# The first unit pair of a two-layer transformer kernel, fed from a transposed copy of x

## The chip, the core and the metric

One core of a Trainium2 chip. The metric is the device time of one execution in microseconds (us), median of several runs. The engines are TensorE (PE, with its weight loads PEld), VectorE (DVE), ScalarE (ACT), GpSimd (POOL) and SyncE (SP), which only issues DMAs here; ScalarE issues DMAs too.

## The reference, cut to what matters

The program is two layers of feed-forward, retention and gated delta rule, cross attention and feed-forward, then a third block, for 256 tokens of width 1024 in float32. What the change touches is the very first sublayer:

```
y = x * rsqrt(mean(x * x, axis=-1) + 1e-6)
u = y * norm_pre[0, 0]
h = (silu(u @ w_gate) * (u @ w_up)) @ w_down      # ffn1, 1024 -> 2816 -> 1024
```

The root belongs to a token (a row of x), the norm's weight ("gain" below) to a column. So u @ w is the token's root times ((x * gain) @ w).

## The kernel before, in words

All weights come as 297 units of 128 x 2048 floats (1 MB). SP loads them in order into a ring of 5 landing buffers (`raw`). Every product is made of three: each operand is split into a high part (`whi`, `uT[0]`, rounded to fp32r) and a low part (the remainder), and high x high, high x low and low x high are added up in PSUM. ScalarE makes a unit's high part (128x2048 copy), POOL its low part in place of the landed unit (four instructions of 128x512, line 391), TensorE multiplies and counts the unit as done, which frees its buffer for SP's next load.

The first feed-forward is worked in chunks of 256 hidden columns. Chunk 0 is one "pair" of units, 0 and 1: the top and bottom 512 rows of 512 columns, 256 of the gate and 256 of the up projection, multiplied by token (TensorE's stationary operand is a block of u, `first_pair`). Bank 0 holds tokens 0 to 127, bank 1 the rest. ScalarE takes Silu of the gate half and VectorE multiplies it with the up half, once per bank (`chunk_by_token`). Chunk 1 follows by rows: `rows_unit` for unit 2 (gate), then `h_transposes` of chunk 0's two products on TensorE, then `rows_unit` for unit 3 (up), then unit 4 (down projection).

Every engine has its instructions in one fixed, hand-written order; semaphores hold them. At the start of the kernel before:

- SP issues x's first token half, the identity, units 0 and 1 in halves with x's second half between them, unit 2, the tables (constants, positions, masks), and units 3 on.
- ScalarE issues the norm's weight as one row, then squares x's first half with a sum per token (`first_root`), takes the root, splits half of unit 0, copies the transposed u (`u_hi`), and so on with the second half; then it splits units 2 and 3, issues five DMAs (three rows, the memory, the small constants), and does chunk 0's Silus with unit 4's split between them.
- VectorE takes the reciprocal, scales x into u (`first_scale`; the norm's row comes spread over 128 partitions from a TensorE product with a row of ones), makes unit 0's low part (`first_lo`, line 1173) and u's low parts (`u_lo`, line 1181).
- POOL skips unit 0 and starts with unit 1.
- TensorE does 9 idle products (line 2247, of zeros, into a bank that is not yet used), the row products (2253), transposes of u (2040), and the pair in parts as the data come (2081, 2098, 2074, 2076, 2088), with 6 idle products between them.

Of the kernel before, what the change touches and what calls it, by code (L numbers as in the profile page):

```python
# [23 lines left out]
P = 128  # L24
# [88 lines left out]

class Prog:
# [19 lines left out]
def build(nc, a, out):  # L134
    ctx = ExitStack()
    with ctx:
# [57 lines left out]
        one_row = arena[0:1, 0:P]  # L194
# [23 lines left out]
        tmpn = view(8240, NT, D)  # L218
# [118 lines left out]
        def _(sp):  # L337
            p = Prog(sp)
            sp.dma_start(x[:, 0, :], a["x"][:, 0, :]).then_inc(sems["x_in0"], 16)
            sp.dma_start(cst[:, 0:P], a["cst"][:, 0:P]).then_inc(sems["ident_in"], 16)  # L340
            for n in range(2):
                for half in range(2):
                    k = slice(half * UNIT // 2, (half + 1) * UNIT // 2)
                    sp.dma_start(raw[n][:, k], a["w"][n][:, k]).then_inc(sems[f"raw_{('first', 'landed')[half]}{n}"], 16)
                if n == 0:
                    sp.dma_start(x[:, 1, :], a["x"][:, 1, :]).then_inc(sems["x_in1"], 16)
            sp.dma_start(raw[2][:], a["w"][2]).then_inc(sems["raw_landed2"], 16)
            sp.dma_start(cst[:, P:], a["cst"][:, P:]).then_inc(sems["tables_in"], 16)
# [3 lines left out]
            for n in range(3, N_UNITS):  # L352
# [11 lines left out]
        def _(pool):  # L364
# [20 lines left out]
            for n in range(N_UNITS):  # L385
                pool.wait_ge(sems["w_hi"], p.count("w_hi"))
                if n == 0:
                    continue
                for c in range(0, UNIT, UNIT // 4):
# [4 lines left out]
                if n == 8:  # L394
                    pool.wait_ge(sems["tables_in"], 48)
                    for i, m in enumerate((UI, UI, LI, LI)):
                        pool.tensor_copy(msk4[:, i, :], m)
                    pool.wait_ge(sems["tables_in"], 48)
# [18 lines left out]
        def _(act):  # L417
# [23 lines left out]
            def row():  # L441

                r = state["row"]
                if r < N_ROWS:
                    if r == 0:
                        act.dma_start(rows[0:1, 0, :], a["rows"][0:1, :]).then_inc(sems["row_landed0"], 16)
                    else:
# [50 lines left out]
            def first_root(t):  # L498

                act.wait_ge(sems[f"x_in{t}"], 16)  # L500
                fn(junk, x[:, t, :], AF.Square, accum_out=st[:, 48 + t:49 + t])
                root(st[:, 54 + t:55 + t], st[:, 48 + t:49 + t], D).then_inc(sems["rms_pre"], 1)
# [55 lines left out]
            def chunk_by_token(u0, c):  # L558
# [5 lines left out]
                for t in range(NT):  # L564
# [4 lines left out]
                    fn(sg[q][:, t * 256:(t + 1) * 256], bank[b[t]][:, 0:256], AF.Silu).then_inc(sems["silu_gate"], 1)  # L569
# [66 lines left out]
            for L in range(DEPTH):  # L636
                base = L * LAYER_UNITS
                if L == 0:
                    first_root(0)
                    first_split(0, (0,))  # L640
                    u_hi(0)
                    first_split(0, (1,))
                    first_root(1)
                    first_split(1)
                    state["split"] = 2
                    u_hi(1)
                    split(2)
# [35 lines left out]
                if L == 0:  # L683
                    act.wait_ge(sems["tables_in"], 48)
# [443 lines left out]
        def _(dve):  # L1128
# [27 lines left out]
            def first_scale(t):  # L1156

                r = st[:, 54 + t:55 + t]
                dve.wait_ge(sems["rms_pre"], p.count("rms_pre"))
                dve.reciprocal(r, r)  # L1160
                dve.drain()
                for h in range(2):
                    c = slice(h * 512, (h + 1) * 512)
                    if t == 0:
                        dve.wait_ge(sems["first_row"], h + 1)
                    stt(ub[:, t, c], bank[2 + h][:, :], r, x[:, t, c], ALU.mult, ALU.mult).then_inc(sems["u_ready"], 1)

            def first_lo(half):

                dve.wait_ge(sems[("w_hi_half", "w_hi")[half]], 1)  # L1170
                for c in range(half * UNIT // 2, (half + 1) * UNIT // 2, UNIT // 4):
                    k = slice(c, c + UNIT // 4)
                    r = tt(wlo[0][:, k], raw[0][:, k], whi[0][:, k].bitcast(F32), ALU.subtract)
                r.then_inc(sems["first_lo"], 1)
# [66 lines left out]
            def ffn(memory=False, tables=None):  # L1241
                for c in range(CH):
                    if c in (0, CH - 1):
                        chunk_by_token(c)
# [5 lines left out]
            def chunk_by_token(c):  # L1250
# [3 lines left out]
                for t in range(NT):  # L1254
                    dve.wait_ge(sems["silu_gate"], p.count("silu_gate"))
                    k = slice(t * 256, (t + 1) * 256)
                    tt(h_tok[q][:, k], sg[q][:, k], bank[b[t]][:, 256:512], ALU.mult).then_inc(sems["ff_product"], 1)
# [26 lines left out]
            dve.memset(one_row, 1.0)  # L1284
            dve.memset(st[:, 0:60], 0.0).then_inc(sems["eps_set"], 1)

            def rotary_angles():

                dve.wait_ge(sems["tables_in"], 48)
                dve.wait_ge(sems["tables_in"], 48)  # L1290
# [44 lines left out]
            for L in range(DEPTH):  # L1335
                base = L * LAYER_UNITS
                if L == 0:
                    state["row"] += 1
                    p.skip("row_landed0", 16)
                    first_scale(0)  # L1340
                    first_lo(0)
                    u_lo(0, 0)
                    u_lo(0, 1)
                    first_lo(1)
                    first_scale(1)
                    u_lo(1, 0)
                    u_lo(1, 1)
                else:
                    boundary()
                ffn(True, None if L else rotary_angles)  # L1350
                if L == 0:
                    dve.wait_ge(sems["trig"], p.count("trig"))
                    ts(sinT[:, :], sinT[:, :], cst[:, C_INV + 1:C_INV + 2], None, ALU.mult)
                boundary()
# [565 lines left out]
        def _(pe):  # L1920
# [40 lines left out]
            def by_rows(b, w, j, parts, start=True, stop=True, low_waited=True):  # L1961
# [3 lines left out]
                for k, c in enumerate(tiles):  # L1965
                    pe.matmul(both, w[0][:, c], parts[:, :, k, :], start=start and k == 0, stop=False)  # L1966
# [6 lines left out]
            def rows_unit(b0):  # L1973
# [956 lines left out]
```

## Time and profile before

| what | us |
|---|---|
| median of 3 runs (lowest, highest) | 1928.16 (1926.05, 1928.46) |
| span of the profiled execution | 1926.1 |
| TensorE busy | 1912.5 (99%) |
| POOL busy | 1545.7 (80%) |
| ScalarE busy | 1081.6 (56%) |
| VectorE busy | 710.4 (37%) |

For the profiled execution the page gives its span and no other time; the three runs stand beside it for comparison. Times inside the trace count from the start of the span. "Chain" is the chain of work that ended last, followed back from the end: each piece is what held up the next. In a timeline, consecutive instructions of one kind are merged; the second figure is from the first one's start to the last one's end.

### The profile page before, as it was taken

How to read it: one execution, taken by the hardware profiler on the slowest of the kernel's cores; microseconds unless marked ns; L12 is line 12 of the kernel's file. 1: busy time of each engine (PE TensorE's matmuls, PEld its weight loads, DVE VectorE, ACT ScalarE, POOL GpSimd, SP SyncE). 2: the span in 40 equal slices, each digit the busy share in tenths (PEclk: the TensorE clock that was granted, in tenths of full speed). 3: DMA queues.
4: the chain of work that ended last, by engine and by line, in shares of the span. 5: the costliest groups of instructions: out<-in, count | busy, mean ns of one | idle time of the engine just before them, and what ended most of it. 6: DMA issues, size and time to landing. Idle time of an engine off the chain costs nothing.

```text
span 1926.1 us, 28361 instructions
## 1 busy us (share of the span) xinstructions
PE 1912.5 (99%) x11293; PEld 1685.0 (87%) x11293; DVE 710.4 (37%) x1428; ACT 1081.6 (56%) x1439; POOL 1545.7 (80%) x1228
## 2 busy tenths in 40 slices
PE   9999999999999999999999999999999999999998
PEld 7888899988888888889999888888999998888887
DVE  2221767521311232128574231113577632122112
ACT  6645684456644575456735565446666667445443
POOL 6998786666899799979776759997767787888995
PEclk9999999999999999999999999999999999999999
DMA  8554543143555565555322535555443444445552
GB/s 321 179 204 175 197 154 132 45 177 130 219 197 183 187 227 205 179 193 186 143 88 105 187 125 207 188 196 202 152 160 145 148 160 153 175 177 206 196 182 103
DMA packets 48661, 331.50 MB, mean 172 GB/s; under 512 B 5393, under 2 KB 6289, under 8 KB 10514
## 3 DMA queue, kind: packets, MB, share of 16 engines
q1 hardware_dynamic: 44208, 314.61, 44.3%
q10 hardware_dynamic: 4322, 15.09, 2.3%
q8 instruction: 89, 1.46, 0.3%
q14 instruction: 42, 0.34, 0.1%
HBM read 328.63 MB, written 1.05 MB: 171 GB/s over the span
## 4 chain that ended last, share of the span: by engine, by line
PE 97%; ACT 1%; DVE 1%; issue 0%; ACTq 0%; DVEq 0%
PE bank L1966 20%; PE bank L1935 16%; PE bank L1936 16%; PE bank L1937 16%; PE bank L1970 10%; PE bank L2074 2%; PE bank L2098 2%; PE bank L2076 1%; PE bank L2412 1%; PE bank L2428 1%; PE bank L2040 1%; PE bank L2534 1%; PE bank L2513 1%; PE bank L2674 1%; PE bank L2088 0%; ACT arena L422 0%
## 5 line engine op out<-in xcount | busy, mean ns | idle before, releaser
L391 POOL TENSOR_TENSOR wlo<-raw,whi 128x512 fp32r<-128x512 f32 x1184 | 1501.0, 1305 | 332.5 <-ACT whi L422 331.9
L422 ACT ACTIVATE whi<-raw 128x2048 fp32r<-128x2048 f32 (+1 forms) x299 | 567.5, 1901 | 188.8 <-PE bank L1937 168.8
L422 ACT ACTIVATE arena<-bank 128x512 f32<-128x512 f32 (+4 forms) x389 | 210.3, 551 | 445.2 <-PE bank L1970 268.4
L1966 PE MATMUL bank<-uT,whi 128*128 128x512 f32 x1632 | 408.2, 392 | 0.0
L1966 PEld LDWEIGHTS bank<-uT,whi 128*128 128x128 f32 x1632 | 296.3, 189 | 55.0
L1970 PEld LDWEIGHTS bank<-uT,wlo 128*128 128x128 f32 x1632 | 222.6, 190 | 15.9
L1970 PE MATMUL bank<-uT,wlo 128*128 128x256 f32 x1632 | 227.6, 282 | 0.0
L1935 PE MATMUL bank<-uT,whi 128*128 128x256 f32 x768 | 222.5, 290 | 0.0
L1936 PE MATMUL bank<-uT,whi 128*128 128x256 f32 x768 | 217.1, 283 | 0.0
L1937 PE MATMUL bank<-uT,wlo 128*128 128x256 f32 x768 | 217.1, 283 | 0.0
L1935 PE MATMUL bank<-whi,uT 128*128 128x512 f32 (+1 forms) x416 | 160.8, 387 | 0.0
L1936 PE MATMUL bank<-wlo,uT 128*128 128x512 f32 (+1 forms) x416 | 158.6, 381 | 0.0
L1937 PE MATMUL bank<-whi,uT 128*128 128x512 f32 (+1 forms) x416 | 158.6, 381 | 0.0
L1935 PE MATMUL bank<-whi,hT_hi 128*128 128x512 f32 x400 | 157.0, 392 | 0.0
L1936 PE MATMUL bank<-wlo,hT_hi 128*128 128x512 f32 x400 | 156.1, 390 | 0.0
L1937 PE MATMUL bank<-whi,hT_lo 128*128 128x512 f32 x400 | 155.8, 389 | 0.0
L1935 PEld LDWEIGHTS bank<-uT,whi 128*128 128x128 f32 x768 | 147.1, 191 | 2.5 <-issue 2.1
L1936 PEld LDWEIGHTS bank<-uT,whi 128*128 128x128 f32 x768 | 147.2, 192 | 1.7 <-issue 1.4
L1937 PEld LDWEIGHTS bank<-uT,wlo 128*128 128x128 f32 x768 | 147.1, 192 | 0.0
L1266 DVE TENSOR_TENSOR bank<-bank,arena 128x512 f32<-128x512 f32 x45 | 31.5, 700 | 312.7 <-ACT arena L422 312.7
L1273 DVE TENSOR_TENSOR bank<-bank,arena 128x512 f32<-128x512 f32 x45 | 31.5, 699 | 190.2 <-ACT arena L422 190.2
L1937 PEld LDWEIGHTS bank<-whi,uT 128*128 128x128 f32 x416 | 78.2, 188 | 15.2
(321 smaller groups left out, 2702.0 us busy)
## 6 DMA issues: line engine op xcount, KB each, us to landing
raw<-in_w SPq DMA_DIRECT2D x295, 1024.0 KB, 4.8
rows<-in_rows ACTq DMA_DIRECT2D x22, 512.0 KB, 4.7
raw<-in_w SPq DMA_DIRECT2D x4, 512.0 KB, 6.7
arena<-in_mem ACTq DMA_DIRECT2D x2, 1024.0 KB, 7.8
x<-in_x SPq DMA_DIRECT2D x2, 512.0 KB, 5.2
arena<-in_amask ACTq DMA_DIRECT2D x1, 576.0 KB, 6.4
out<-x SPq DMA_DIRECT2D x1, 512.0 KB, 2.7
out<-arena SPq DMA_DIRECT2D x1, 512.0 KB, 2.7
```

What stands on the lines that cost most here:

```text
L391: r = pool.tensor_tensor(wlo[n % LAND][:, k], raw[n % LAND][:, k], whi[n % RING][:, k].bitcast(F32), ALU.subtract)
L422: return act.activation(o, i, f, **k)
L1266: tt(gate, gate, gate_low, ALU.add).then_inc(sems["gate_sum"], 1)
L1273: tt(up, up, up_low, ALU.add)
L1935: pe.matmul(o, l[0], r[0], start=start, stop=False)
L1936: pe.matmul(o, l[0], r[1], start=False, stop=False)
L1937: return pe.matmul(o, l[1], r[0], start=False, stop=stop)
L1966: pe.matmul(both, w[0][:, c], parts[:, :, k, :], start=start and k == 0, stop=False)
L1970: r = pe.matmul(both[:, 0], w[1][:, c], parts[:, 0, k, :], start=False, stop=stop and k == KT - 1)
L2040: r = pe.transpose(bank[b][:, k * P:(k + 1) * P], ub[:, t, f:f + P], ident)
L2074: pe.matmul(bank[b][:, :], u, w[0][:, c], start=half == 0 and k == 0, stop=False)
L2098: r = pe.matmul(bank[b][:, :], uT[1][:, 4 * half + k, t * P:(t + 1) * P], w[0][:, k * 512:(k + 1) * 512], start=False, stop=half == 1 and ...
```

## The change: what it does

A second copy of x, transposed (columns on partitions) with the norm's gain in 8 columns ahead of it, is laid out by the host as an input `xT`. The pair of units 0 and 1 is multiplied with x times gain, split into high and low parts in the buffer of the memory's transposes (`mT`), for both token banks at once. The token's root is applied to the pair's results: as the scale of Silu and as a factor of the product with the up half. The sum of squares is formed from the squares of xT: added up over the 8 column blocks on VectorE, then over partitions by TensorE products with ones, once per token down the partitions and once as a row spread over all of them (`row_root`). With that row VectorE forms u (transposed, in place), ScalarE copies its high part and VectorE subtracts for its low part, in four steps (`first_u`, `first_u_hi`); unit 2's first pass waits for each step. POOL now makes the low part of the second halves of units 0 and 1, VectorE that of the first halves. x itself is loaded after the tables. The 16 transposes of u, the row products and the 6 idle products between are gone; 13 idle products stand at the start in place of 9.

```diff
 # SP
+            sp.dma_start(x_turned[:, 0:cut], a["xT"][:, 0:cut]).then_inc(sems["turned_in0"], 16)
+            first_weights(0)
+            sp.dma_start(x_turned[:, cut:], a["xT"][:, cut:]).then_inc(sems["turned_in1"], 16)
+            first_weights(1)
+            sp.dma_start(cst[:, 0:2 * P], a["cst"][:, 0:2 * P]).then_inc(sems["ident_in"], 16)
+            for n in range(2, 4):
+                sp.dma_start(raw[n][:], a["w"][n]).then_inc(sems[f"raw_landed{n}"], 16)
...
+            for t in range(NT):
+                sp.dma_start(x[:, t, :], a["x"][:, t, :]).then_inc(sems["tables_in"], 16)
 # POOL
-                if n == 0:
-                    continue
-                for c in range(0, UNIT, UNIT // 4):
+                for c in range(UNIT // 2 if n < 2 else 0, UNIT, UNIT // 4):
 # ScalarE
+            def first_values(half):
+                act.wait_ge(sems[f"turned_in{half}"], 16)
+                for k in range(4 * half, 4 * half + 4):
+                    fn(mT[0][:, k, :], xs[:, k, :], AF.Identity, scale=x_gain[:, k:k + 1]).then_inc(sems["start_act"], 1)
...
+            def first_roots():
+                act.wait_ge(sems["act_bank2"], p.count("act_bank2"))
+                eps = st[:, 60:61]
+                fn(st[:, 54:56], bank[3][:, 0:4:2], AF.Sqrt, scale=1.0 / D, bias=eps).then_inc(sems["start_act"], 1)
+                fn(row_root, bank[2][:, 0:SEQ], AF.Sqrt, scale=1.0 / D, bias=eps).then_inc(sems["start_act"], 1)
+            def first_u_hi():
+                for j in range(4):
+                    act.wait_ge(sems["start_dve"], START_DVE[f"x_scaled{j}"])
+                    fn(uT[0][:, 2 * j:2 * j + 2, :], xs[:, 2 * j:2 * j + 2, :], AF.Copy).then_inc(sems["start_act"], 1)
...
-                    first_root(0)
+                    first_values(0)
                     first_split(0, (0,))
-                    u_hi(0)
+                    first_squares(0)
                     first_split(0, (1,))
-                    first_root(1)
+                    first_values(1)
+                    first_squares(1)
                     first_split(1)
                     state["split"] = 2
-                    u_hi(1)
-                    split(2)
+                    first_roots()
+                    split()
+                    first_u_hi()
+                    split()
 # VectorE
+            def squares_added():
+                s = x_squares
+                dve.wait_ge(sems["start_act"], START_ACT["squares1"])
+                tt(s[:, 4:6], s[:, 4:6], s[:, 6:8], ALU.add)
+                dve.drain()
+                tt(s[:, 0:2], s[:, 0:2], s[:, 4:6], ALU.add)
+                dve.drain()
+                tt(s[:, 0], s[:, 0], s[:, 1], ALU.add).then_inc(sems["start_dve"], 1)
+            def first_u():
+                def scaled(j):
+                    for k in (2 * j, 2 * j + 1):
+                        r = stt(xs[:, k, :], xs[:, k, :], x_gain[:, k:k + 1], row_root, ALU.mult, ALU.mult)
+                    r.then_inc(sems["start_dve"], 1)
+                def lo(j):
+                    k = slice(2 * j, 2 * j + 2)
+                    dve.wait_ge(sems["start_act"], START_ACT[f"u_hi{j}"])
+                    tt(uT[1][:, k, :], xs[:, k, :], uT[0][:, k, :].bitcast(F32), ALU.subtract).then_inc(sems["start_dve"], 1)
+                dve.wait_ge(sems["start_act"], START_ACT["roots"])
+                dve.reciprocal(row_root, row_root)
+                dve.reciprocal(st[:, 54:56], st[:, 54:56]).then_inc(sems["start_dve"], 1)
+                dve.drain()
+                scaled(0)
+                for j in range(1, 4):
+                    scaled(j)
+                    lo(j - 1)
+                lo(3)
...
+                    first_values_lo(0)
                     first_lo(0)
+                    dve.wait_ge(sems["start_act"], START_ACT["squares0"])
+                    tt(x_squares[:, 0:2], x_squares[:, 0:2], x_squares[:, 2:4], ALU.add)
+                    first_values_lo(1)
+                    squares_added()
                     first_lo(1)
+                    first_u()
 # TensorE
+            def first_unit_pair(banks):
+                def product(n, w, values, ks, tiles=(0, 1), stop=False):
+                    for t in tiles:
+                        for k in ks:
+                            r = pe.matmul(bank[banks[t]][:, :], values[:, 4 * n + k, t * P:(t + 1) * P], w[:, k * 512:(k + 1) * 512],
+                                          start=w is whi[0] and values is mT[0] and k == 0, stop=stop and k == ks[-1])
+                    return r
+                pe.wait_ge(sems["start_act"], START_ACT["value3"])
+                pe.wait_ge(sems["w_hi_half"], 1)
+                product(0, whi[0], mT[0], (0, 1))
...
+                product(1, whi[1], mT[0], (0, 1))
+                pe.wait_ge(sems["ident_in"], 16)
+                pe.wait_ge(sems["start_dve"], START_DVE["squares_added"])
+                for t in range(NT):
+                    pe.matmul(bank[3][:, 2 * t:2 * t + 2], x_squares[:, 0, t * P:(t + 1) * P], ones[:, 0:2], start=True, stop=True)
+                pe.matmul(bank[2][:, 0:SEQ], ones, x_squares[:, 0, :], start=True, stop=True).then_inc(sems["act_bank2"], 1)
+                pe.wait_ge(sems["start_dve"], START_DVE["values_lo1"])
+                product(1, whi[1], mT[1], (0, 1))
...
                 for k, c in enumerate(tiles):
+                    if first and k % 2 == 0:
+                        pe.wait_ge(sems["start_dve"], START_DVE[f"u_lo{k // 2}"])
                     pe.matmul(both, w[0][:, c], parts[:, :, k, :], start=start and k == 0, stop=False)
...
-            idle_products(9)
-            pe.wait_ge(sems["row_landed0"], 16)
+            idle_products(13)
```

`first_values_lo(half)` is four VectorE instructions of 128x256, (x * gain) - high part, each waiting for its value. `START_ACT` and `START_DVE` are tables of counts of the two start semaphores.

## Rows read from the trace of the kernel before

**Rows 1.** The page: busy shares, TensorE's granted clock, the chain by engine.
```profile
PE 1912.5 (99%) x11293; PEld 1685.0 (87%) x11293; DVE 710.4 (37%) x1428; ACT 1081.6 (56%) x1439; POOL 1545.7 (80%) x1228
...
PEclk9999999999999999999999999999999999999999
...
PE 97%; ACT 1%; DVE 1%; issue 0%; ACTq 0%; DVEq 0%
```
**Rows 2.** The chain of waits, first 45 us: start, us, what.
```profile
1.71 4.21 PE bank L2247 x9
...
26.47 1.81 PE bank L1966 x8
28.29 0.95 PE bank L1970 x8
...
32.03 0.44 PE bank L2192 x4
32.47 1.85 PE bank L1966 x8
```
**Rows 3.** ScalarE's timeline to 34 us: start, us, engine, line, operation, out<-in, count.
```profile
4.86 1.06 ACT L422 ACTIVATE arena<-x 128x1024 f32<-128x1024 f32 x1 [2.06 <-DMA x<-in_x]
...
20.13 1.92 ACT L422 ACTIVATE whi<-raw 128x2048 fp32r<-128x2048 f32 x1
20.63 0.36 ACTq L448 DMA_DIRECT2D rows<-in_rows  x1
21.03 0.93 ACTq L651 DMA_DIRECT2D arena<-in_mem  x1
...
21.99 1.50 ACTq L448 DMA_DIRECT2D rows<-in_rows  x2
23.52 1.23 ACTq L655 DMA_DIRECT2D small<-in_small  x1
24.78 1.28 ACT L422 ACT_TABLE_LOAD   x1 [0.93 <-issue]
26.08 0.39 ACT L422 ACTIVATE arena<-bank 128x256 f32<-128x256 f32 x1
26.36 1.91 ACT L422 ACTIVATE whi<-raw 128x2048 fp32r<-128x2048 f32 x1
28.16 0.37 ACT L422 ACTIVATE arena<-bank 128x256 f32<-128x256 f32 x1
```
**Rows 4.** Line 344's two loads of unit 1's halves, issued at 3.05 and 3.55.
```profile
L344 SPq DMA_DIRECT2D raw<-in_w x2: 452/487/522, 3.1 to 3.6; - x2
...
DMA to landing us min/median/max: 7.9/8.3/8.6
```
**Rows 5.** VectorE's groups by line and form, whole span: count | busy us, mean ns.
```profile
L1266 DVE TENSOR_TENSOR bank<-bank,arena 128x512 f32<-128x512 f32 x45 | 31.5, 700 | 312.7 <-ACT arena L422 312.7
...
L1173 DVE TENSOR_TENSOR wlo<-raw,whi 128x512 fp32r<-128x512 f32 x4 | 2.6, 686 | 0.3 <-ACT whi L422 0.3
...
L1627 DVE RECIPROCAL st<-st 128x2 f32<-128x2 f32 x8 | 1.3, 166 | 13.5 <-ACT arena L422 13.5
...
L1305 DVE SCALAR_TENSOR_TENSOR bank<-arena,bank 128x256 f32<-128x256 f32 x3 | 1.3, 429 | 0.2
...
L1464 DVE RECIPROCAL gat<-gat 128x16 f32<-128x16 f32 x2 | 0.5, 246 | 0.0
```
**Rows 6.** ScalarE's groups by line and form, whole span: copies with a column scale.
```profile
L422 ACT ACTIVATE arena<-arena,st 128x256 f32<-128x256 f32 x16 | 7.3, 503 | 0.9 <-DVE st L1627 0.9
```
**Rows 7.** POOL's line 391 to 22 us: ns min/median/max, first and last start.
```profile
L391 POOL TENSOR_TENSOR wlo<-raw,whi x4: 1282/1290/1305, 16.6 to 20.3; 128x512 fp32r<-128x512 f32 x4
```
**Rows 8.** VectorE's line 1774 and POOL's line 391 from 1506 us on, as rows 7.
```profile
L1774 DVE TENSOR_TENSOR arena<-arena x2: 693/1241/1789, 1506.2 to 1506.8; 128x512 f32<-128x512 f32 x2
...
L391 POOL TENSOR_TENSOR wlo<-raw,whi x4: 1610/1738/1760, 1506.5 to 1511.4; 128x512 fp32r<-128x512 f32 x4
```
**Rows 9.** Line 448, the rows' DMA issues, whole span: as rows 7.
```profile
L448 ACTq DMA_DIRECT2D rows<-in_rows x22: 334/352/845, 20.6 to 1741.9; - x22
```

More of the change, by code:

```diff
@@ L111, in rope_tables @@
     return np.concatenate([np.concatenate([cos, cos]), np.concatenate([-sin, sin])], axis=1).astype(np.float32)
+START_ACT = {f"value{k}": k + 1 + k // 4 for k in range(KT)}
+START_ACT.update(squares0=5, squares1=10, roots=12, u_hi0=13, u_hi1=14, u_hi2=15, u_hi3=16)
+START_DVE = {"values_lo0": 1, "weights_lo0": 2, "values_lo1": 3, "squares_added": 4, "weights_lo1": 5, "recip": 6}
+START_DVE.update(x_scaled0=7, x_scaled1=8, u_lo0=9, x_scaled2=10, u_lo1=11, x_scaled3=12, u_lo2=13, u_lo3=14)
 class Prog:
@@ L568, in chunk_by_token @@
                         act.wait_ge(sems["unit_done"], u0 + (1, 29)[c // (CH - 1)] + 1)
-                    fn(sg[q][:, t * 256:(t + 1) * 256], bank[b[t]][:, 0:256], AF.Silu).then_inc(sems["silu_gate"], 1)
+                    first = u0 == 0 and c == 0
+                    if first and t == 0:
+                        act.wait_ge(sems["start_dve"], START_DVE["recip"])
+                    fn(sg[q][:, t * 256:(t + 1) * 256], bank[b[t]][:, 0:256], AF.Silu,
+                       scale=st[:, 54 + t:55 + t] if first else 1.0).then_inc(sems["silu_gate"], 1)
                     if c == 0 and t == 0:
@@ L1168, in first_lo, with first_values_lo @@
[L1168 to L1174, printed above, removed]
+            def first_values_lo(half):
+                for k in range(4 * half, 4 * half + 4):
+                    dve.wait_ge(sems["start_act"], START_ACT[f"value{k}"])
+                    r = stt(mT[1][:, k, :], xs[:, k, :], x_gain[:, k:k + 1], mT[0][:, k, :].bitcast(F32), ALU.mult, ALU.subtract)
+                r.then_inc(sems["start_dve"], 1)
@@ L1239, in lo_parts, with ffn @@
                        ALU.subtract).then_inc(sems[f"dve_read{b}"], 1)
-            def ffn(memory=False, tables=None):
+            def ffn(memory=False, tables=None, first=False):
                 for c in range(CH):
                     if c in (0, CH - 1):
-                        chunk_by_token(c)
+                        chunk_by_token(c, first and c == 0)
                     else:
@@ L1959, in proj_T, with by_rows @@
                 r.then_inc(sems["unit_done"], 1)
-            def by_rows(b, w, j, parts, start=True, stop=True, low_waited=True):
+            def by_rows(b, w, j, parts, start=True, stop=True, low_waited=True, first=False):
                 both = bank[b].rearrange("p (a b) -> p a b", a=2)
@@ L2126, in first_pair @@
[L2126 to L2147 removed]
+                    first_unit_pair(banks)
@@ new lines, in first_pair @@
+                    return
+                wa = unit()
+                acquire(a, readers[0])
+                hi_phase(wa, a, 0, 0)
+                lo_phase(wa, a, 0, 0)
+                m = state["unit"]
+                state["unit"] += 1
+                wb = whi[m % RING], wlo[m % LAND]
+                pe.wait_ge(sems["w_hi"], m + 1)
+                hi_phase(wb, a, 0, 1, True)
+                weights_lo_phase(wb, a, 0, 1, False)
+                lo_phase(wb, a, 0, 1).then_inc(sems["tok_half"], 1)
@@ L2249, in _ @@
             pe.wait_ge(sems["eps_set"], 1)
-            idle_products(9)
-            pe.wait_ge(sems["row_landed0"], 16)
-            for h in range(2):
-                pe.matmul(bank[2 + h][:, :], one_row, rows[0:1, 0, h * 512:(h + 1) * 512], start=True, stop=True)\
-                    .then_inc(sems["first_row"], 1)
+            idle_products(13)
             for L in range(DEPTH):
@@ L2870, in pack @@
     assert n == N_UNITS
+    turned = f["x"][0].T.reshape(KT, P, SEQ).transpose(1, 0, 2).reshape(P, KT * SEQ)
+    gain = f["norm_pre"][0, 0].reshape(KT, P).T
     tiled = lambda m: np.ascontiguousarray(m.reshape(NT, P, D).transpose(1, 0, 2))
     arrays = {
-        "w": w, "small": small, "rows": np.stack(rows), "x": tiled(f["x"][0]), "mem": tiled(f["mem"][0]),
+        "w": w, "small": small, "rows": np.stack(rows), "x": tiled(f["x"][0]), "xT": np.concatenate([gain, turned], axis=1), "mem": tiled(f["mem"][0]),
         "pos": np.ascontiguousarray(f["positions"][0:1]), "cst": shape_constants(), "lvl": level_masks(),
```

152 lines of the change are left out of this document (60 added, 92 removed).

## Prediction

> **What bounds the kernel now.** I read the page's busy shares and chain first, then the chain of waits over the first 45 us, then ScalarE's timeline there. TensorE is busy 99% of the span and holds 97% of the chain [rows 1]. So whatever ends TensorE's first stretch earlier or later moves the end by as much, as long as no later wait swallows it; the question is only at which time TensorE begins steady work. The chain says when: the first unit pair ends and unit 2 begins at 26.47; unit 2 takes 5.56 (two passes of 1.81 and 0.95) and ends at 32.03; four transposes of chunk 0's product take 0.44; unit 3 begins at 32.47 [rows 2]. In all of it TensorE waits for almost nothing, because it was given the pair, the transposes of u and idle products in turn. I use 32.47, the start of unit 3, as the mark: behind it TensorE runs without waiting, so the shift of that start is the shift of the end.
>
> The second thing to see is ScalarE. It splits units 2 and 3, then its queue issues five DMAs (20.63 to 24.75), then it loads the Silu table (24.78, 1.28) and only then reads the pair's first result at 26.08; the split of unit 4 comes between the two Silus, so the second starts at 28.16 [rows 3]. TensorE asks for that second product at 32.03, so this string has 3.5 us of cover now. The change takes the cover and the start of the string in different directions.
>
> **The change part by part.** *Arrivals.* x's first half was read at 4.86 [rows 3]; xT's first half stands in its place with 8 columns more, so 4.9. The last half of raw 1 was issued at 3.55 and landed 8.6 later, at 12.2 [rows 4]; the bytes ahead of it stay the same but for the identity (64 KB later), so it stays at 12.2. Units 2 and 3 come ahead of the tables on SP's queue now and x itself behind them; unit 4 stands behind some 1 MB more than before, but ScalarE asks for it only at 34.0 below, and x and the tables are first read after several units more. Unit 5's load waits for unit 0's end, which comes earlier (13.6).
>
> *ScalarE, first part.* Four scaled copies of 128x256 (a lone one is 0.50 [rows 6]; in a row I take 0.42, the second starting before the first's end is recorded): 4.95 to 6.6. Then half-split, squares, half-split at 1.0 each (1.06 recorded [rows 3]) to 9.6; four copies more to 11.3; squares to 12.3; the halves of unit 1 to 13.3 and 14.3.
>
> *POOL* now also splits half of units 0 and 1: two instructions of 1.29 [rows 7] from 9.75, two from 14.4. Before, it did nothing until 16.6, and VectorE did its low half at 0.69 apiece undisturbed [rows 5, 7].
>
> *VectorE against POOL.* The new VectorE work has both operands in SBUF. What that costs beside POOL [rows 8]: of two equal additions the first took 0.69, the second 1.79, while POOL's four weight instructions of 1.29 took 1.61 to 1.76. The two take turns, one instruction each: a VectorE instruction waits for the running POOL one (1.25), and POOL for it (0.3 to 0.5). One whose operand is in PSUM kept 0.70 over 45 cases with POOL busy [rows 5]. The Trainium skill ("SBUF — State Buffer", Who interferes with whom) has it as an exclusive lock on a shared port, which the instruction that starts first keeps to its end. Read that way alone, a VectorE string without gaps would keep POOL out and pay nothing in the u stage below, and the sum would be an estimated +0.4; the turn-taking [rows 8] says otherwise, and I follow the rows.
>
> *Sum of squares.* The low parts of values 4 to 7 alternate with POOL's two and end at 13.6. The three additions (0.6, 0.6, 0.35 and drains) would end at 14.1; POOL's unit-1 instructions fall among them, and with two turns the last ends at 16.4. The products with ones (two of 2 columns and one of 256, full f32) I put at 1.1 with start and tail, two ScalarE roots 0.6: 18.3. *Unit 2's split* is queued behind the roots on ScalarE, so the added wait for the sums holds it and, behind it, POOL's unit 2: 1.9 [rows 3], 20.2.
>
> *Reciprocal of 256 elements:* no row. From 2 to 16 elements it grows from 0.166 to 0.246, 5.7 ns an element [rows 5], so 1.6; the lower bound is an ordinary 128x256 instruction, 0.43 [rows 5], the upper some 2.1. I take 1.5: 20.2 with the small one 20.4. It hardly counts, for POOL starts unit 2 at 20.3 in either case.
>
> *The u stage.* Eight scalings (0.35) and four subtractions (0.6) are 5.2 alone. POOL's four instructions of unit 2 stand between the first: four turns of 1.25 + 0.25 bring the second scaled pair to 26.4; free of POOL, the rest gives u_lo0 27.0, x_scaled3 29.0, u_lo3 30.4.
>
> *TensorE.* Thirteen idle products at 0.468 (4.21 for nine [rows 2]), fewer if the clock rises among them: about 7.5. Groups of four at 0.91 follow the data: unit 0 done 13.6, the sums 17.6, the pair 22.1, which is 4.3 earlier than 26.47. Unit 2's first pass then waits for u_lo0 to u_lo3, 27.1 to 31.0, and 0.95 + 1.84 + 0.95 bring its end to 34.7 (32.03 before).
>
> *The string behind it.* The sequencer can't issue its DMAs until x_scaled3 lets the last u_hi go: 29.1. Their price: 4.12 in this trace [rows 3]; 1.9 if each takes what later ones take (a rows issue: 0.352 median [rows 9], 0.46 for mem). The rows issues were slow only behind a loaded start, and at 29 us units 4 and 5 are in; I take rows at 0.35 and keep the first-time 0.93 and 1.23: 3.2, to 32.3. Table 1.28, Silu 0.39: 34.0; unit 4's split to 35.9; Silu 36.2; product and transposes, 0.9: unit 3 at about 36.9, against 32.47: **+4.4** (at 1.9, unit 2's own end and Silu give +3.4; at 4.1, +5.3). The skill ("ScalarE: Activation LUTs", What ACT_TABLE_LOAD costs) adds a drain of about 1.38 us to each load, which would make it an estimated +5.8; by the trace [rows 3] Silu starts 0.02 after the load's end, and I add none.
>
> *Behind the mark* POOL is next: it splits unit 4 until 41.9, TensorE asks at 42.5; unit 5 and on are needed later still. Nothing given back, nothing more lost. The second silu's scale and the two-operand product cost as before; leaving out 16 transposes, the row product and the broadcast saves TensorE time that it then spends waiting. POOL's tables wait at unit 8 is long past.
>
> **Forecast:** 4.4 us later. The profiled span is 1926.1 [rows 1], 2.1 under the median of the runs, inside their spread of 2.4; on the median, 1928.2 + 4.4 = **1932.6**.
>
> **Rivals.** (1) *The turns don't bite*: POOL and VectorE mostly miss each other. Then the sums are ready at 15.6, x_scaled3 at 22.1, unit 2 ends at 27.9, the DMAs at 25.4, the second Silu at 29.5, unit 3 at 29.9: -2.6 (-1.6 to -3.5 by the price of the issues), 1925.6: not slower. For it: a turn lost or won moves a whole instruction. Against: POOL has work at exactly those times. It decides at u_lo0: the change breaks even where that comes at 22.6, 4.4 before my 27.0. (2) *The head's whole gain comes through*: the pair ends at 20.1, unit 2 follows without stall and the Silus are in time: -6.4, 1921.8. For it: the pair's work itself shrinks so far. Against: the DMAs and the table stand ahead of the Silu at any time after the last u_hi. (3) *TensorE's clock*: the nine idle products of 0.468 us ran at the 1.2 GHz level and unit 2's at 0.226 at the 2.4 GHz level [rows 2], though the page's granted clock reads full throughout [rows 1], so its row doesn't show the start. TensorE now idles from 22.1 to 27.1; should the clock fall back there, unit 2 costs up to 4 more, of which 2.3 is hidden behind the Silu string: +6 to +8, 1935. (The skill, "TensorE: Matmul & The Clock Gate", Part 1, says that an idle stretch returns the clock to half; no row here shows one.)
>
> **How the numbers follow.** Forecast 0.61, rival 1 0.15, rival 2 0.12, rival 3 0.12. 0.2%, about what a measurement of this kernel can tell from no change, is 3.9 us. Of the forecast's share 0.43 lies above that (its own range is +3 to +6, 1931 to 1934.5) and 0.18 within; with rival 3 slower is 0.55; with rival 1 the same is 0.33; rival 2 makes faster 0.12. The range goes from rival 1's better end to rival 3's middle: 1925 to 1936, with rival 2 and the worst of rival 3 left out, near 0.17.
>
> **What would show it.** Right: VectorE's first scalings at 1.3 us or more each with POOL's unit-2 instructions at 1.5; a TensorE wait of about 5 us ahead of unit 2; the Silu table load after 31; unit 3's start near 37. Wrong: u_lo0 before 23, or the table load before 27 (rival 1); unit 2 directly behind a pair that ends at 20 (rival 2); matmuls of 0.46 apart after the wait (rival 3).

## The result, and the profile after

| kernel | unit 3 starts | unit 4 starts | span | median (lowest to highest, runs) | ratio to before |
|---|---|---|---|---|---|
| before | 32.47 | 38.07 | 1926.1 | 1928.16 (1926.05 to 1928.46, 6) | |
| after | 38.04 | 43.63 | 1931.5 | 1933.82 (1933.31 to 1934.01, 6) | 1.0033 [1.0022, 1.0044] |

The change makes the kernel slower by 0.33%, 4.2 to 8.5 us by the interval; the two profiled executions differ by 5.4. Forecast were 1932.6 and +4.4. The executions of the kernel before fall into two groups, near 1926.4 and near 1928.3 (a few near 1936, in two sets of the experiments, pull the ratios there down a little), and the profiled one, with its span of 1926.1, belongs to the second, so that differences of less than 2 us are read below from the marks in the traces and not from medians.

The page of after, as [rows 1]:
```profile
PE 1909.2 (99%) x11277; PEld 1682.6 (87%) x11277; DVE 726.9 (38%) x1443; ACT 1085.7 (56%) x1445; POOL 1546.8 (80%) x1228
...
PE 96%; DVE 2%; ACT 1%; issue 0%; DMA 0%; ACTq 0%; DVEq 0%; SPq 0%
```
TensorE is busy for 3.3 us less in a span that is 5.4 longer: its work shrank, and it waits. The chain after, as [rows 2], says on what:
```profile
1.17 5.88 DMA raw<-in_w
...
13.92 0.60 DVE arena L1210
...
14.59 1.78 DVE arena L1212
...
16.45 1.34 DVE arena L1214
...
17.92 0.58 PE bank L2171 x4
...
19.73 1.75 DVE arena L1228
...
21.60 5.77 DVE arena L1220 x4
...
34.39 0.47 ACT arena L434
34.86 1.80 ACT whi L434
36.67 0.37 ACT arena L434
...
37.06 0.49 DVE arena L1319
...
37.60 0.44 PE bank L2267 x2
38.04 1.85 PE bank L2032 x8
```
Read it from the end: unit 3 (L2032) follows the transposes (L2267), these chunk 0's second product (L1319), that the second Silu, the split of unit 4, the first Silu, the table load, the DMA issues. All of this stands behind VectorE: three additions of squares (L1210 to L1214), the reciprocal row (L1228), four scalings (L1220) that take 1.44 each. Before, TensorE held nearly all of this stretch [rows 2].

ScalarE's timeline after, as [rows 3], and POOL's, to the end of unit 2's low part:
```profile
30.20 0.38 ACTq L458 DMA_DIRECT2D rows<-in_rows  x1
30.61 0.45 ACTq L686 DMA_DIRECT2D arena<-in_mem  x1
...
31.09 1.15 ACTq L458 DMA_DIRECT2D rows<-in_rows  x2
32.27 0.74 ACTq L690 DMA_DIRECT2D small<-in_small  x1
33.09 1.28 ACT L434 ACT_TABLE_LOAD   x1 [0.47 <-issue]
34.39 0.47 ACT L434 ACTIVATE arena<-bank,st 128x256 f32<-128x256 f32 x1
```
```profile
10.12 2.73 POOL L403 TENSOR_TENSOR wlo<-raw,whi 128x512 fp32r<-128x512 f32 x2 [9.68 <-ACT whi L434]
14.55 2.94 POOL L403 TENSOR_TENSOR wlo<-raw,whi 128x512 fp32r<-128x512 f32 x2 [1.71 <-ACT whi L434]
21.58 5.51 POOL L403 TENSOR_TENSOR wlo<-raw,whi 128x512 fp32r<-128x512 f32 x4 [4.09 <-ACT whi L434]
```
The slow additions and the four slow scalings lie exactly beside POOL's second and third group. TensorE's waits (us in total, times, longest), and in the second fence, the engines' busy times in stretches of 2 us (each with its count; the last three numbers are TensorE's granted clock, the DMA share and GB/s):
```profile
PE bank L2032 <- DVE uT L1226: 4.7, 2, 4.5
PE bank L2171 <- DVE arena L1214: 2.9, 1, 2.9
```
```profile
24.00:26.00 2.00, 0.00 (x0) 0.00 (x0) 2.00 (x3) 0.63 (x1) 2.00 (x3) 1.00 1.01 422
26.00:28.00 2.00, 0.00 (x0) 0.00 (x0) 2.00 (x3) 0.59 (x1) 1.09 (x1) 0.70 1.00 418
28.00:30.00 2.00, 1.77 (x3) 1.00 (x4) 2.00 (x5) 0.67 (x2) 0.00 (x0) 0.50 0.45 188
30.00:32.00 2.00, 1.83 (x5) 0.89 (x4) 1.45 (x3) 1.80 (x2) 0.00 (x0) 0.50 0.34 102
32.00:34.00 2.00, 2.00 (x11) 1.81 (x10) 0.00 (x0) 1.53 (x2) 1.30 (x2) 0.59 0.97 266
```
The forecast's mechanism and that of its rival 3 are both there: the clock fell to its 1.2 GHz level (0.50) in the idle stretch and stayed there until the second half of unit 2. Which of the two sets unit 3, the trace alone leaves close: unit 2 ends at 36.9, the product at 37.55, and TensorE waits 0.4 for it.

### The profile page after: what moved, and what is told of

Read it like the earlier page. It is cut to its first block, busy times and chain, and to the rows that moved or that the text cites. A ratio compares the mean times of both kernels' runs of the same rounds, so it can differ in the third digit from the quotient of the medians.

```text
span 1931.5 us, 28352 instructions
## 1 busy us (share of the span) xinstructions
PE 1909.2 (99%) x11277; PEld 1682.6 (87%) x11277; DVE 726.9 (38%) x1443; ACT 1085.7 (56%) x1445; POOL 1546.8 (80%) x1228
## 4 chain that ended last, share of the span: by engine, by line
PE 96%; DVE 2%; ACT 1%; issue 0%; DMA 0%; ACTq 0%; DVEq 0%; SPq 0%
PE bank L2032 20%; PE bank L1999 16%; PE bank L2000 16%; PE bank L2001 16%; PE bank L2036 10%; PE bank L2140 2%; PE bank L2198 2%; PE bank L2142 1%; PE bank L2483 1%; PE bank L2499 1%; PE bank L2106 1%; PE bank L2605 1%; PE bank L2584 1%; PE bank L2745 1%; ACT arena L434 1%; PE bank L2188 0%
## 5 line engine op out<-in xcount | busy, mean ns | idle before, releaser
L2032 PE MATMUL bank<-uT,whi 128*128 128x512 f32 x1632 | 410.7, 393 | 4.8 <-DVE uT L1226 4.7
L2032 PEld LDWEIGHTS bank<-uT,whi 128*128 128x128 f32 x1632 | 296.9, 189 | 61.6 <-issue 4.9
L1331 DVE TENSOR_TENSOR bank<-bank,arena 128x512 f32<-128x512 f32 x45 | 31.5, 700 | 312.7 <-ACT arena L434 312.7
L1338 DVE TENSOR_TENSOR bank<-bank,arena 128x512 f32<-128x512 f32 x45 | 31.5, 699 | 189.2 <-ACT arena L434 189.2
L2001 PEld LDWEIGHTS bank<-whi,uT 128*128 128x128 f32 x416 | 78.2, 188 | 15.2
```

Source lines behind the costliest of these rows:

```text
L1331: tt(gate, gate, gate_low, ALU.add).then_inc(sems["gate_sum"], 1)
L1338: tt(up, up, up_low, ALU.add)
L2001: return pe.matmul(o, l[1], r[0], start=False, stop=stop)
```

## The experiments

Theory: VectorE's turns with POOL delay u, and the string on ScalarE behind u (DMA issues, table load, Silu, unit 4's split, Silu) sets unit 3. The clock rival (the prediction's rival 3): the fall of the clock is the loss. The no-turns rival (akin to its rival 1): the turns are not what costs. All kernels are the changed one with the edit shown; line numbers shift by a few. "Rest" is the span less unit 4's start: 1888.0 before, 1887.9 after. The ratio is to runs of the kernel before taken beside each (in sets 1 to 4, 5 to 7, 8 and 9, 10 and 11, and 12), whose medians went from 1926.80 to 1928.24; medians of different sets are compared by it alone.

| | edit | unit 3 | unit 4 | rest | median | ratio to before, 95% |
|---|---|---|---|---|---|---|
| 1 | idle products behind the pair | 38.86 | 44.46 | 1887.8 | 1933.82 | 1.0033 [1.0021, 1.0046] |
| 2 | POOL waits for u | 38.98 | 44.58 | 1887.9 | 1933.90 | 1.0035 [1.0022, 1.0049] |
| 3 | u stage in PSUM | 33.39 | 38.99 | 1887.9 | 1929.92 | 1.0013 [1.0003, 1.0023] |
| 4 | DMAs and table early | 38.70 | 44.29 | 1888.0 | 1934.08 | 1.0035 [1.0023, 1.0048] |
| 5 | 4 and 1 | 36.91 | 43.34 | 1888.4 | 1933.38 | 1.0022 [1.0011, 1.0033] |
| 6 | 3, squares in PSUM | 31.94 | 37.54 | 1889.2 | 1928.35 | 0.9997 [0.9986, 1.0009] |
| 7 | 6 and 4 | 31.10 | 37.48 | 1889.5 | 1928.90 | 0.9997 [0.9986, 1.0008] |
| 8 | squares in PSUM alone | 36.61 | 42.20 | 1889.2 | 1933.16 | 1.0031 [1.0018, 1.0043] |
| 9 | 6, other order | 32.23 | 37.82 | 1889.3 | 1928.72 | 1.0007 [0.9998, 1.0016] |
| 10 | idle products in all waits | 37.73 | 43.32 | 1888.0 | 1933.16 | 1.0028 [1.0017, 1.0039] |
| 11 | 9, idle products | 31.14 | 36.73 | 1889.2 | 1927.72 | 1.0002 [0.9993, 1.0011] |
| 12 | 11, eight drains | 31.11 | 36.71 | 1888.4 | 1926.86 | 0.9998 [0.9989, 1.0007] |

**1: the clock.**
```diff
                 product(1, wlo[1], mT[0], (2, 3), (1,), True).then_inc(sems["unit_done"], 1)
+                for _ in range(18):
+                    pe.matmul(bank[4][:, :], run[:, 0, 0:P], run[:, :, :], start=True, stop=True)
```


> The changed kernel with 18 idle products of 128x512 (into bank 4, not yet used) behind the first pair, so that TensorE does not stand idle from 23.6 to 28.1. Theory (VectorE's turns with POOL set the end through ScalarE's string of DMA issues, table and Silu; the half-rate clock from 26.8 to 33.6 is hidden behind that string): the granted clock stays at its full level, unit 2 ends near 35 instead of 36.9, TensorE then waits for chunk 0's second product, unit 3 starts at 38.0 as in the changed kernel, total within 0.5 us of it (1933.8). Rival (the clock's fall is what costs): unit 3 starts near 36, total about 2 us lower.


The clock did not stay full; it fell earlier, in the wait of 2.9 for the sums, and made the products with ones and the pair slow, so that the scalings began 0.9 later:
```profile
18.00:20.00 2.00, 2.00 (x7) 1.82 (x8) 0.98 (x2) 0.00 (x0) 0.00 (x0) 0.50 1.04 387
```
Unit 2 then ran at full clock, and TensorE waited 1.1 for the product. The string came last, as the theory says, but with u late the test was not clean; the tenth run repeats it.

**2: POOL holds back.** VectorE has the SBUF to itself until u is done.
```diff
+                if n == 2:
+                    pool.wait_ge(sems["start_dve"], START_DVE["u_lo3"])
```


> The changed kernel, but POOL waits with unit 2's low part until the last part of u is done. Theory (turns): the eight scalings take 0.4 to 0.5 each instead of 1.4, x_scaled3 comes near 25.7 instead of 30.2 and u_lo3 near 27.2 instead of 31.5; now POOL's unit 2 (27.3 to 32.4) holds unit 2's low products, its end is near 36, unit 3 starts near 36.6: about 1.4 us below the changed kernel. Rival (turns cost nothing, the scalings are slow for another reason): the scalings stay at 1.4, unit 2 ends later than 36.9, total 2 to 5 us above the changed kernel.


```profile
21.38 1.67 DVE arena L1222 x4
...
27.38 4.96 POOL wlo L405 x4
32.39 2.08 PE bank L2038 x8
34.46 3.13 PE bank L2034 x8
```
The same four scalings take 1.67 without POOL, against 5.77: the turns are the cost. The wait that swallowed the gain was expected: unit 2's low pass (L2038) waits 3.9 for POOL, which ends at 32.3 (expected 32.4). What was not expected is the clock, 0.50 from 28 to 36: the three passes behind that wait took 6.2 in place of 3.7 (0.95, 1.84 and 0.95), and unit 2 ended at 38.5, not 36.

**3: the u stage in PSUM.** Both engines work at once, but each scaling has only one tensor operand in SBUF: the reciprocal row and the scaled x stand in PSUM, and ScalarE copies from there.
```diff
-                        r = stt(xs[:, k, :], xs[:, k, :], x_gain[:, k:k + 1], row_root, ALU.mult, ALU.mult)
+                        r = stt(u_parts[j][:, k % 2, :], xs[:, k, :], x_gain[:, k:k + 1], bank[2][:, 0:SEQ], ALU.mult, ALU.mult)
...
-                    tt(uT[1][:, k, :], xs[:, k, :], uT[0][:, k, :].bitcast(F32), ALU.subtract)
+                    tt(uT[1][:, k, :], u_parts[j], uT[0][:, k, :].bitcast(F32), ALU.subtract)
...
-                dve.reciprocal(row_root, row_root)
+                dve.reciprocal(bank[2][:, 0:SEQ], row_root)
```


> The changed kernel with the u stage through PSUM: the reciprocal row and the scaled x are written to PSUM banks, so each scaling and each subtraction has one operand in SBUF and one in PSUM; POOL does unit 2 at the same time as before. Theory (turns happen only where both operands are in SBUF): scalings 0.4 to 0.5, POOL's four at 1.29 each, u_lo3 near 27.2, unit 3 near 33.7, total about 4.3 us below the changed kernel: 1929.5. Rival (the two engines slow each other whatever the operands): scalings stay above 1 us and the total stays within 1 us of 1933.8.


```profile
21.40 1.66 DVE L1221 SCALAR_TENSOR_TENSOR bank<-arena,bank 128x256 f32<-128x256 f32 x4
```
```profile
21.34 5.01 POOL L404 TENSOR_TENSOR wlo<-raw,whi 128x512 fp32r<-128x512 f32 x4 [4.09 <-ACT whi L435]
```
Side by side, neither pays: 1.66 and 5.01 (5.77 and 5.51 after). Unit 3 comes 4.65 earlier, and the median is 3.9 under that of run 1, taken beside it. This refutes the no-turns rival.

**4: the string earlier.** DMAs issued and the table loaded (by a Silu on one column) while ScalarE waits for u; both Silus ahead of unit 4's split.
```diff
-                    if c == 0 and t == 0:
+                    if c == 0 and t == (1 if first else 0):
...
-                    first_u_hi()
-                    split()
...
+                    fn(st[:, 62:63], st[:, 60:61], AF.Silu)
+                    first_u_hi()
+                    split()
```


> The changed kernel with only ScalarE's string moved: the five DMAs are issued right behind unit 2's split, the Silu table is loaded there by a Silu of one column, and chunk 0's second Silu comes ahead of unit 4's split. The u stage and its turns with POOL stay (u_lo3 near 31.5). Theory: the second product is ready near 34 instead of 37.6, and now the end of unit 2 decides, which the half-rate clock puts at 36.9: unit 3 at 37.4, total about 0.7 us below the changed kernel. Rival (the string alone is the cost): unit 3 near 34.5, total 3.5 us lower.


Both Silus were done at 34.2, but unit 3 came 0.7 later than in the changed kernel, not 0.6 earlier:
```profile
18.05 0.79 PE bank L2172 x4
18.84 1.08 PE bank L2173 x2
...
22.46 5.78 DVE arena L1221 x4
...
31.68 2.07 PE bank L2033 x4
33.76 1.71 PE bank L2037 x8
...
38.70 1.84 PE bank L2033 x8
```
Two things came together. The clock fell behind the wait for the sums already, as in 1 (0.57 from 18 to 20, 1.00 in the changed kernel): the products with ones took 0.79 and 1.08 in place of 0.58 and 0.55, and the scalings began at 22.46 in place of 21.60. And with the string out of the way TensorE's own path ends last: u's last part, then unit 2 at the lower clock, with eight low products in 1.71 (0.95 in [rows 2]). What the string alone costs, this run doesn't show.

**5: both**, 4 with the idle products of 1.

> The string moved as in e4, and the 18 idle products of e1 as well. Theory: the clock's fall, hidden in e1, now counts: with it gone unit 2 ends near 35, unit 3 starts near 35.4, total about 2 us below e4 and 2.6 below the changed kernel: 1931.2. Rival (the clock never costs anything): as e4.


Unit 2 ran from 29.0 to 36.3 at full clock, and unit 3 came 1.1 earlier than in the changed kernel, though not at 35.4: here too the clock fell behind the wait for the sums (0.58 from 18 to 20), and the scalings began 0.3 later. So the two paths are nearly equally long, and where only one was cured (1, 4) nothing was gained; but both of those were set back by the early fall of the clock as well. Of the 1.1, 0.8 went in a wait of unit 4 for POOL's low part.

**6: squares in PSUM too.**
```diff
-                fn(x_squares[:, k, :], xs[:, k, :], AF.Square)
+                o = psum[:, 6:8, :] if half else x_squares[:, k, :].rearrange("p (a c) b -> p a (c b)", a=2)
+                fn(o, xs[:, k, :].rearrange("p (a c) b -> p a (c b)", a=2), AF.Square)
...
-                tt(s[:, 4:6], s[:, 4:6], s[:, 6:8], ALU.add)
+                tt(s[:, 2:4].rearrange("p a b -> p (a b)"), s[:, 0:2].rearrange("p a b -> p (a b)"), bank[6], ALU.add)
...
```


> e3, and the second half of the squares goes to PSUM as well, so that the additions for the sum of squares each have one PSUM operand at most beside one in SBUF. Theory: the last addition ends near 15.6 instead of 17.8, everything behind the sums moves 2 us ahead of e3: unit 3 near 31.7, total about 6.3 below the changed kernel and 0.6 below the one before: 1927.5. Rival (the sums wait for the data, not for POOL): as e3.


```profile
14.11 0.69 DVE L1213 TENSOR_TENSOR arena<-arena,bank 128x512 f32<-128x512 f32 x1
14.87 0.43 DVE L1215 TENSOR_TENSOR bank<-arena,bank 128x256 f32<-128x256 f32 x1
...
15.70 0.42 DVE L1218 TENSOR_TENSOR arena<-arena,bank 128x256 f32<-128x256 f32 x1
```
No addition loses a turn, the clock stays at 1.00, and unit 4 starts 0.5 before that of the kernel before. Unit 3 came at 31.94, as expected (31.7). The time doesn't show it: the rest is 1.2 longer (see 12).

**7: with the string of 4.**

> e6 with the string moved as in e4: no turns in the u stage and the sums, no DMA issue or table load ahead of the Silus. Theory: TensorE's own work decides: the pair ends near 21.5, unit 2 near 29, unit 3 starts near 29.4, 3 us before the kernel before: total 1925.1. Rival (something else, as the pair's data or the bandwidth taken by the earlier row loads, sets the end): no better than e6.


Unit 3 came 0.8 earlier than in 6, not 2.5; it was u itself, then unit 2, that ended last, and unit 4 waited 0.8 for POOL, whose unit 3 began late (27.3), behind ScalarE's copies of u. In the time, no better than that of 6, this run's rival held.

**8: squares alone in PSUM.**

> The second half of the squares in PSUM alone, everything else as in the changed kernel (the reciprocal row and the scaled x stay in SBUF). My theory says that the sums and the four scalings each lost whole instructions to POOL, and that ScalarE's string sets the start of unit 3. Then the last addition ends at about 16.1 (17.8 in the changed kernel), the scalings still take some 1.45 us each beside POOL, the string comes some 1.5 us earlier, unit 3 starts at 36.5 (38.0) and the time is about 1.5 lower, 1932.3. The rival, that the end of unit 2 at the lower clock is what sets unit 3, says that unit 3 moves by less than 0.7 or follows unit 2's end, wherever the clock puts that.


```profile
15.42 0.42 DVE arena L1217
...
19.80 5.64 DVE arena L1223 x4
```
Additions end at 15.8, the four scalings still take 5.64 and unit 3 comes 1.43 earlier, though the clock fell here too (0.50 from 26 to 32). With 3 (4.65) that makes 6.08; the two together in 6 gave 6.10: the turns in the sums and those in the u stage add up. Here and in 6 it is the string that ends last; in 3 the product was there at 32.7, and unit 2, at a clock of 0.52 to 0.63, ended 0.2 after it.

**9: another order.** Unit 3's split ahead of u's copies, Silus ahead of unit 4's split, DMAs behind.

> Squares and u stage in PSUM as in the sixth experiment, with another order on ScalarE: unit 3's split directly behind unit 2's, then the copies of u's high parts, both Silus, unit 4's split, and the five DMA issues behind that. My theory says that with the turns gone what sets unit 3 is this string and what sets unit 4 is POOL's wait for unit 3's split. With both out of the way unit 3 should start at 30.3 to 31.1 (32.47 before), POOL should begin unit 3 at about 24.9 in place of 27.3 and later, and unit 4 should start at 36.5 (38.07 before): about 1.5 under the kernel before at that mark, of which 1.0 is lost in the third block if the wait of the sixth and seventh experiments comes again, so 1926.6 to 1927.6. The rival says that something else, the landing of units 4 to 7 or POOL, gives the gain back before unit 6, and the time stays at that of the kernel before, 1928.2.


POOL ran through units 2 to 4 without a pause, and the Silus were done at 27.5. But unit 3 came at 32.23, not at 30.3 to 31.1: unit 2 took until 31.8, at half the clock from 26 to 28:
```profile
26.00:28.00 2.00, 2.00 (x8) 1.74 (x8) 0.89 (x3) 1.99 (x4) 2.00 (x2) 0.50 1.03 430
```
**10: the first, repeated cleanly**: ten idle products ahead of the sums, eighteen behind the pair, three behind each pair of unit 2's first six products.

> The changed kernel with idle products of zeros in all of TensorE's waits before unit 3: ten ahead of the sums, eighteen behind the pair, three each behind the second, fourth and sixth product of unit 2 (all into banks whose contents nobody uses at that time). The clock should then be full from 7 us on, and unit 2 end at 34.9 (36.9 in the changed kernel). My theory says that the changed kernel's fall of the clock cost nothing, since ScalarE's string sets the product of chunk 0 at 37.5: unit 3 still starts at 37.8 to 38.1 and the time stays at 1933.8 within 0.4. The rival, that the clock's fall is a part of the loss, says that unit 3 comes up to 2.0 earlier, 36.0, and the time is 1932.


```profile
36.22 0.38 PE L2274 MATMUL bank<-cst,arena 128*128 128x128 f32 x2
37.29 0.44 PE L2274 MATMUL bank<-cst,arena 128*128 128x128 f32 x2 [0.69 <-DVE arena L1319]
```
The string of the same run, from the chain:
```profile
32.17 0.52 ACTq L690
...
36.35 0.37 ACT arena L434
```
The clock was 1.00 throughout; unit 2 ended 0.6 earlier (2.0 were expected; the idle products themselves held its last high products by 0.5), and TensorE waited 0.69 for the product, 0.4 in the changed kernel. Unit 3 gained 0.31, and all of it came down the string: its last DMA issue ended at 32.7 in place of 33.0, its second Silu at 36.72 in place of 37.04. So the run shows no part of the changed kernel's loss as the clock's: the clock rival's mechanism is there, and hidden.

**11: the order of 9, clock kept** by eight idle products ahead of and within unit 2.

> The order of the ninth experiment with idle products in the waits ahead of and within unit 2: four behind the pair, two each behind unit 2's second and fourth product. In the ninth, the granted clock was 0.50 from 25 to 29 us, behind three waits of 0.6 to 1.0, and unit 2 ended at 31.8 with ScalarE's string done at 27.5. If the clock is what that order lost, it should be full here throughout, unit 2 end at 30.0, unit 3 start at 30.4 (32.2 in the ninth, 32.47 before), unit 4 at 36.0 (38.07 before), and the time be 1.8 under the ninth's: about 1927, or 1926 if the third block's wait of 1.0 stays away. The rival, that something else held unit 2 or that the gain is given back at units 5 to 7 (landing, POOL), says that the time stays within 0.7 of the ninth's.


Clock at 1.00, unit 3 at 31.14, 1.09 earlier than in 9; the span is 1.2 shorter. Where the string is out of the way, what the clock costs unit 2 (1.1 here) is paid in full. The expected 1.8 was too much: u's last part still holds unit 2 until 26.2.

**12: the 1.2 in the rest.** Runs 6, 7, 8, 9 and 11 share it. TensorE's waits and VectorE's timeline of 11, in the third block:
```profile
PE bank L2675 <- DVE arena L1775: 1.0, 1, 1.0
```
```profile
1352.06 0.22 DVE L1733 TENSOR_TENSOR arena<-bank,small 128x64 f32<-128x64 f32 x1 [2.70 <-PE bank L2668]
1352.76 1.16 DVE L1736 SCALAR_TENSOR_TENSOR arena<-arena 128x64 f32<-128x64 f32 x1 [0.47 <-issue]
```
The multiplication stands 0.47 on "issue", and then loses a turn to POOL.
```diff
                     first_u()
+                    for _ in range(8):
+                        dve.drain()
```


> The eleventh experiment with eight drains more on VectorE behind u's last low part, where it waits some 5 us for chunk 0's Silu; nothing else differs. In the five kernels with the squares in PSUM VectorE's queue stands 0.45 to 0.47 on issue ahead of the 128x64 multiplication of the third block's step sizes, which then takes 1.15 to 1.17 in place of 0.25 to 0.28 and makes TensorE wait 1.0; none of the other eight kernels has it, and the five have the same number of VectorE instructions ahead of it. If it is the place of that instruction in VectorE's program that brings the gap, eight instructions more move the gap into the 2.7 us for which VectorE waits for TensorE there: the multiplication takes about 0.26, the wait of 1.0 is gone, the time from unit 4's start to the end is 1887.9 in place of 1889.2, the span 1924.6 and the time about 1.2 under the eleventh's, 1926.5. The rival, that the gap comes from when the instruction falls against POOL or the transfers, says that the wait stays and the time is the eleventh's, 1927.7.


```profile
1352.42 0.23 DVE L1735 TENSOR_TENSOR arena<-bank,small 128x64 f32<-128x64 f32 x1 [2.70 <-PE bank L2670]
1352.75 0.27 DVE L1738 SCALAR_TENSOR_TENSOR arena<-arena 128x64 f32<-128x64 f32 x1
```
Gap, lost turn and wait are gone and the span is 0.8 shorter; the ratio moves the same way, inside its interval. So the gap goes with a place in VectorE's program (five kernels with the same number of instructions ahead of it have it, the other eight and this one don't), and this loss is not a matter of the first units' work. Why there is a gap at that place is not shown. Of the rest 0.4 is left over that of the kernel before, 0.3 of it a new wait at L2120. The span is 1.0 under that of before; by the runs the two can't be told apart.

## Why the prediction was right, and where its sizes were off

| step | forecast | measured |
|---|---|---|
| last addition of squares | 16.4 | 17.78 |
| roots | 18.3 | 19.71 |
| second scaled pair | 26.4 | 27.37 |
| last u_hi can go | 29.0 | 30.17 |
| unit 2's end | 34.7 | 36.9 |
| DMAs issued | 32.3 | 33.0 |
| second Silu | 36.2 | 37.04 |
| unit 3 | 36.9 | 38.04 |

**The bound and the mark.** Unit 3's shift of 5.57 and the span's of 5.4 agree to 0.2, and so does the rest (1888.0 and 1887.9). Next to nothing is given back behind the mark, as forecast. That the profiled span lies 2.1 under the median was no matter of spread: in every run on record the span is 1.8 under the time. The sum doesn't hang on it.

**The turns.** Right in place and size: two in the additions cost 1.2 and 1.0 (1.78 and 1.33, of 0.60 and 0.35), four in the scalings 1.44 each with POOL's at 1.38 (forecast 1.5 and 1.5). The lock of the Trainium skill ("SBUF — State Buffer", Who interferes with whom) is there, but VectorE's four scalings, which followed one another without a gap, did not keep POOL out: the engines alternated (5.77 beside 5.51). The rows that the forecast took [rows 8] told it rightly. The prediction's rival 1 (the turns don't bite) is refuted by the changed kernel's own trace, where u's first low part ended at 28.0 and the rival needed 22.6, and by 2, 3 and 8.

**The mis-sized term is the end of the sums.** "The three additions (0.6, 0.6, 0.35 and drains) would end at 14.1" doesn't follow from low parts that end at 13.6; 13.6 and 1.6 is 15.2, and with the two turns 17.5. It measured 17.78; the low parts themselves ended 0.3 later, since unit 0's first half landed at 7.05 and ScalarE waited 0.49 for it, a wait that the forecast didn't have. Everything behind the sums hangs on them: moved on by these 1.1, the forecast's own terms put unit 3 at 38.0, and it measured 38.04. That the agreement is so close is partly luck: DMA issues were 0.4 cheaper than forecast (2.8), the low parts 0.3 later, the Silus with a scale 0.1 dearer each (0.47 for 0.39 [rows 3]); the reciprocal row (1.75, forecast 1.5) counts little, since POOL and VectorE start side by side behind it (21.58 and 21.60). Three smaller sums are off as well: 16.4, 1.1 and 0.6 make 18.1 and not 18.3, 18.3 and 1.5 make 19.8 and not 20.2, and 36.2 and 0.9 make 37.1 and not 36.9.

**The string** (issue, table, Silu, split, Silu) is what sets unit 3: 10 shows it. But the forecast had the string and, as its rival 3, the fall of TensorE's clock as alternatives with a chance each; both came together. Rival 3 put up to 4 on unit 2. Of the 2.2 by which unit 2 ended late, u's last part brings 1.1 (31.5 for 30.4); the other 1.1 is the clock's, an estimate from the passes at full clock in [rows 2]. By 10, none of that reached unit 3. The Trainium skill's rule ("TensorE: Matmul & The Clock Gate", Part 1), that an idle stretch returns the clock to half, agrees with the trace: 1.00 until 26, 0.50 from 28 on, behind an idle stretch from 23.6. The wait of 2.9 for the sums left it at 1.00 in the same trace.

**The prediction's rival 2**, the head's whole gain of 6.4, failed at its own condition: unit 2 can't follow the pair without u, and u came 4.5 later than the pair's end. With the turns gone, the string reordered and the clock kept (12), 1.4 at unit 4 is what was had.

## What to carry to other kernels

When a step is moved behind a product, look first at what the moved work runs beside: four VectorE instructions with both tensors in SBUF took 5.77 beside POOL and 1.66 with one of them and the result in PSUM, and everything queued behind them moved along. Where two paths end within a microsecond of each other, take both away before calling either innocent, and look whether the cure itself moved something else: 1 and 4 alone came out 0.8 and 0.7 later at unit 3, together (5) 1.1 earlier, and in all three the clock also fell ahead of u, where it had not fallen before. And compare the rest of the program by itself: a few instructions more in one engine's program cost some 1 us at a place 1300 us later.

## What the runs showed of the hardware that was not expected

- The granted clock fell at different places in programs that differ little, and in these runs the length of a wait alone doesn't tell where. In the changed kernel it fell in an idle stretch of 4.5 (0.50 from 28 to 32). The wait of 2.9 for the sums brought it down in runs 1, 4 and 5 and left it at 1.00 in the changed kernel and in 2 and 3. In unit 2's three waits it fell in 3 (waits of 0.43, 0.59 and 0.65) and in 9 (1.04, 0.59, 0.65), and it stayed at 1.00 in 6 (0.57, 0.59, 0.65) and in 7 (0.93, 0.58, 0.65). The page's row of 40 slices reads 9 throughout in the changed kernel and in 1, 3, 6, 7 and 9.
- A reciprocal of 128x256 takes 1.75 into SBUF and 1.75 into PSUM, as much as four scalings of that size (1.66).
- VectorE's queue stood 0.45 to 0.47 on issue at one instruction in five kernels; eight drains ahead of it moved the gap away. What makes it was not tried.
